# The slot lists of all but five expert steps from a table in device memory, in a one-core mixture-of-experts encoder step

## The chip, the cores and the metric

The kernel runs on one core of a Trainium2 chip. The metric is the device time of one launch in microseconds (us). The three runs of the kernel before took 1218.28, 1220.01 and 1220.52 us, median 1220.01.

## What is computed

One layer of a streaming encoder for 384 tokens: 256 prompt frames and 8 running streams of 16 frames, width 1024, all in float32. An attention mixer with three branches comes first (latent attention, forgetting attention, memory attention, with gates), then a mixture of experts, which this change is about:

```
scores = sigmoid(t @ w_router);  sel = scores + router_bias
top 4 of 8 groups, then the top 8 of the 64 experts in them; w = scores / sum * 2.5
routed = sum over experts e of  gate[:, e] * ((silu(t @ w_gate[e]) * (t @ w_up[e])) @ w_down[e])
y = LayerNorm(ALPHA * x1 + routed + shared expert)
```

Each of the 384 tokens goes to 8 of the 64 experts (hidden width 256), so an expert has 48 tokens in the mean.

## The kernel before, in words

**Order.** `plan()` writes out by hand the order of everything up to the shared expert: projections, attention units, merge, first layer norm, router, shared expert. Each engine walks through this one list and takes its own part. The expert steps come after it, written out in each engine's block. Engines meet only through semaphores.

**Expert steps.** The 64 experts are done two at a time in 32 steps (`PAIRS`), 64 slots for each expert, one slot for each PSUM row. A 33rd step (number `PAIRS`, "quad") takes four chunks of 32 slots for experts with more than 64 tokens; `FIXED` is 33. Further quad steps run only if more than four chunks are needed (`if_more`), which is not so for these inputs. A step n does this:

- **SyncE** (`load_pair`, L608) loads gate, up and down weights of step n, six transfers of 1 MB, into one of two buffer sets. The loads of step n+2 go out, each kind as soon as step n is done with its buffer.
- **GpSimd** (`gather`, L770) fetches the 128 token rows of a step from `x1_dram` with one indirect DMA, whose row numbers are a column of `idx`. It waits on `idx_ready` for that column.
- **TensorE** (`step`, L1198): gate and up products (L1206), the transposes of the rows of the next step (`turn`, L1195), two transposes of the hidden tile (L1213; they wait for `hid_ready`), six products that bring the previous step's result back to token order (L1220), then `slot_tokens` for step n+3 (L932), then the down products (L1231).
- **ScalarE** (`pair`, L1383): silu (L1385), and the scaled copy of the down products (L1390).
- **VectorE** (`pair`, L1833): the hidden tile (L1837), the copies of the transposed rows (`take_turned`, L1831), the copy of the transposed hidden tile (L1841), six additions into `x_sb` (L1858), the matrix `back` (L1845 to L1847), then `copy_slots(n + 3)` (L1580 to L1587) and `build_onehot(n + 4)` (L1566 to L1573).

**Slot lists.** Before a step can gather, it must know which token and which weight sits in each of its 128 slots. Routing gives for each token and expert a position within the expert (`rep`, from `("V", "pos")`). `tgp` holds for each token and expert three numbers: token + 1, weight, position - 1. For step n, `build_onehot` copies the two columns of the step and compares an iota with the position, once for each of the three token tiles; `slot_tokens` multiplies that one-hot matrix with the columns, which sums to the token and weight of each slot; `copy_slots` turns the result into `idx` and `info`. The list of step n+3 is made inside step n. Lists 0 and 1 are made in the plan's `slots` pieces, between those of the shared expert, list 2 just before the loop. `more_chunks` works out which experts need further chunks, and `more_columns` adds their columns to `tgp` (L1556 to L1560).

**Loop.** Steps 0 to 27 run in hardware loops of two steps a turn (`Fori(0, EARLY)`, `EARLY` is 14), the others are unrolled.

Of the kernel before, what the change touches and what calls it, by code (L numbers as in the profile page):

```python
# [33 lines left out]
P = 128  # L34
# [3 lines left out]
TT = 3  # L38
# [14 lines left out]
COLS = E + MORE + 16  # L53
# [14 lines left out]
for _n, _w in (("ident", 128), ("tri", 128), ("ones", 256), ("blk", 128), ("strict", 128), ("causal", 128),  # L68
               ("wfox", 240), ("stack", 64), ("rope", 96), ("iota", MORE), ("tok", 3),
               ("oh", 8), ("eps", 1), ("unused", 1), ("chunks", 10), ("before", 64)):  # L70
    CST[_n] = (_c, _w)
    _c += _w
# [7 lines left out]
def constants():  # L80

    c = np.zeros((P, NCST + T + NMASK), np.float32)
# [9 lines left out]
    masks[:, T + H * 256:] = np.repeat(np.eye(8), P, axis=1)  # L92
# [31 lines left out]
    put("before", np.broadcast_to((np.arange(8)[None, :] < np.arange(8)[:, None]).reshape(1, 64), (P, 64)))  # L124
    return c
# [142 lines left out]
def build(nc, a, outs):  # L268
# [34 lines left out]
    with ExitStack() as ctx:  # L303
# [34 lines left out]
        idx = ctx.enter_context(nc.sbuf_tensor("idx", [P, 8], I32))  # L338
        table = ctx.enter_context(nc.sbuf_tensor("table", [1, 96], I32))
# [104 lines left out]
        counts, chunks, first, more_n = (N.take(1) for _ in range(4))  # L444
        over = N.take(10)
        offs = N.take(MORE)
        since, is_in, begun, shift = (N.take(MORE) for _ in range(4))
        pcol = [N.take(TT, 12) for _ in range(2)]
# [26 lines left out]
        gates_dram = nc.dram_tensor("gates", (GATES, P, T), F32, kind="Internal").ap()  # L475
        x1_dram = nc.dram_tensor("x1_rows", (T, D), F32, kind="Internal").ap()
# [77 lines left out]
        tgp_cleared = sem("tgp_cleared")  # L554
# [4 lines left out]
        more_step = sem("more_step")  # L559
# [47 lines left out]
        def _(sp):  # L607
# [137 lines left out]
        def _(pool):  # L745
# [40 lines left out]
            with pool.Fori(0, EARLY) as i:  # L786
# [17 lines left out]
        def _(pe):  # L804
# [122 lines left out]
            def slot_tokens(n, par, quad=False):  # L927

                w = 12 if quad else 6
# [6 lines left out]
            def more_chunks(k):  # L936
# [6 lines left out]
                elif k == 1:  # L943
                    pe.wait_ge(chunks_ready, 1)
                    mm(ps["S"][1][0:E, 0:1], cc("strict")[0:E, 0:E], chunks[0:E, :], start=True, stop=True).then_inc(chunks_done, 1)
                else:
                    pe.wait_ge(begun_ready, 1)
                    mm(ps["S"][1][:, 0:MORE], cc("ones")[0:E, 0:P], shift[0:E, :], start=True, stop=True)
# [249 lines left out]
            def step(n, q, loaded, quad=False, turned=None, listed=False, lists=None):  # L1198
# [12 lines left out]
                pe.wait_ge(idx_ready, n + 3 if lists is None else lists)  # L1211
# [11 lines left out]
                if listed:  # L1223
                    slot_tokens(n + 3, 1 - q, quad or (isinstance(n, int) and n + 3 >= PAIRS))
# [16 lines left out]
            with pe.Fori(0, EARLY) as i:  # L1241
                for q in range(2):
                    step(i * 2 + q, q, [(q, 32 * (i + 1))], turned=i + 1 + q, listed=True)
            for n in range(2 * EARLY, PAIRS):
                step(n, n % 2, [(n % 2, 32 * (n // 2 + 1))], turned=(n + 1) // 2 + 1, listed=n + 3 < FIXED, lists=min(n + 3, FIXED))
            step(PAIRS, 0, [(0, 32 * (PAIRS // 2 + 1)), (1, 32 * (PAIRS // 2 + 1))], quad=True, lists=FIXED)
            with if_more(pe):
                for n in range(FIXED, FIXED + 2):
                    slot_tokens(n, n % 2, True)
                turn(FIXED, FIXED % 2, FIXED // 2 + 1)  # L1250
                slot_tokens(FIXED + 2, FIXED % 2, True)
# [678 lines left out]
```

## Time and profile before

| | us |
|---|---|
| median of three runs | 1220.01 |
| the profiled execution, its time | 1219.02 |
| its span, first to last instruction | 1216.8 |
| expert steps, first gate product to the last down product | 616.5 to 1193.8 |

The page gives for each engine its busy time and share of the span. TensorE's products are busy for 97% of it, VectorE for 43%, ScalarE for 16%, GpSimd for 4%. The mean granted clock of TensorE is 0.992 of full speed, and 308.95 MB were moved by the 16 DMA engines, 380 GB/s of it in the expert steps. On the chain of work that ended last, TensorE holds 93%. In all rows times are microseconds from the start of the span; "idle before" in square brackets is the time the engine stood still ahead of the instruction, with what ended it.

### The profile page before, as it was taken

The numbers are of one execution on the slowest core, as the hardware profiler recorded it, in microseconds if no ns is written. First come the engines' busy times: TensorE is split into PE (matmuls) and PEld (weight loads), VectorE is DVE, ScalarE is ACT, GpSimd is POOL, SyncE is SP. The second block draws the span as 40 slices with busy tenths as digits, with TensorE's granted clock in tenths as the row PEclk, the third lists the DMA queues.
The fourth block names the chain that finished last, engine by engine and source line by source line (L and its number), as shares of the span: only waits on it lengthen the run. The fifth ranks groups of instructions, "written<-read, shape, count | busy, mean of one in ns | idle before, by whom it ended". The sixth has DMA issues, their size and how long they took to land.

```text
span 1216.8 us, 17670 instructions
## 1 busy us (share of the span) xinstructions
PE 1174.9 (97%) x6510; PEld 678.3 (56%) x6510; DVE 524.6 (43%) x1455; ACT 199.4 (16%) x365; POOL 46.2 (4%) x55
## 2 busy tenths in 40 slices
PE   6999999999999997999999999999999999999994
PEld 4454546666666664545755555555555555555551
DVE  1231014444555642325745445544554454445436
ACT  0212024344433320000100011011101110110011
POOL 0100000000000000001100000000000000000000
PEclk9999999999999998999999999999999999999997
DMA  8431152222264437874259999999999999999981
GB/s 290 143 125 70 69 185 99 80 89 89 89 215 148 156 117 250 333 309 148 84 201 386 382 376 378 400 367 369 380 396 373 379 380 399 378 378 384 375 331 53
DMA packets 84212, 308.95 MB, mean 254 GB/s; under 512 B 14152, under 2 KB 25968, under 8 KB 58040
## 3 DMA queue, kind: packets, MB, share of 16 engines
q1 hardware_dynamic: 67328, 274.96, 57.6%
q0 software_dynamic: 5696, 15.47, 4.4%
q10 hardware_dynamic: 11136, 17.83, 4.2%
q8 instruction: 32, 0.52, 0.2%
q14 instruction: 20, 0.16, 0.0%
HBM read 302.20 MB, written 10.74 MB: 257 GB/s over the span
## 4 chain that ended last, share of the span: by engine, by line
PE 93%; DVE 3%; DMA 1%; issue 0%; ACT 0%; ACTq 0%; DVEq 0%
PE ps_P L1206 19%; PE ps_P L923 10%; PE ps_V L1231 10%; PE ps_V L1220 9%; PE ps_P L829 6%; PE ps_V L1142 5%; PE ps_S L1220 5%; PE ps_T L822 4%; PE ps_P L837 3%; PE ps_V L1151 3%; PE ps_T L1195 3%; PE ps_S L932 2%; PE ps_V L891 1%; PE ps_P L964 1%; PE ps_V L1183 1%; PE ps_S L852 1%
## 5 line engine op out<-in xcount | busy, mean ns | idle before, releaser
L1206 PE MATMUL ps_P<-arena,branch_out 128*64 128x256 f32 (+1 forms) x2176 | 233.6, 379 | 0.6 <-DVE branch_out L1831 0.6
L1206 PEld LDWEIGHTS ps_P<-arena,branch_out 128*64 128x64 f32 (+1 forms) x2176 | 151.2, 135 | 91.0 <-issue 19.2
L923 PE MATMUL ps_P<-xT,weight_ring 128*128 128x384 f32 x384 | 137.0, 491 | 0.0
L1837 DVE TENSOR_TENSOR branch_out<-branch_out,ps_P 128x256 f32<-128x256 f32 x33 | 13.9, 421 | 266.2 <-PE ps_P L1206 266.2
L1220 PE MATMUL ps_V<-weight_ring,branch_out 128*128 128x512 f32 x264 | 124.2, 593 | 0.0
L1231 PE MATMUL ps_V<-arena,branch_out 128*64 128x512 f32 (+1 forms) x544 | 120.6, 599 | 0.0
L1390 ACT ACTIVATE weight_ring<-ps_V,merge 128x512 f32<-128x512 f32 x66 | 45.3, 687 | 427.6 <-PE ps_V L1231 427.6
L1858 DVE TENSOR_TENSOR x_sb<-x_sb,ps_V 128x512 f32<-128x512 f32 x136 | 93.4, 687 | 22.8 <-PE ps_V L1220 17.4
L923 PEld LDWEIGHTS ps_P<-xT,weight_ring 128*128 128x128 f32 x384 | 68.3, 191 | 37.2 <-issue 3.1
L1220 PEld LDWEIGHTS ps_V<-weight_ring,branch_out 128*128 128x128 f32 x264 | 48.0, 192 | 47.3 <-issue 47.3
L1142 PE MATMUL ps_V<-branch_out,weight_ring 128*128 128x384 f32 x192 | 64.1, 497 | 7.4 <-DVE merge L1776 7.0
L1231 PEld LDWEIGHTS ps_V<-arena,branch_out 128*64 128x64 f32 (+1 forms) x544 | 34.8, 135 | 59.5 <-issue 58.9
L1220 PE MATMUL ps_S<-weight_ring,branch_out 128*128 128x512 f32 x132 | 67.4, 592 | 0.0
L829 PE MATMUL ps_P<-weight_ring,xT 128*128 128x512 f32 (+1 forms) x144 | 61.3, 586 | 4.8 <-DMA weight_ring<-w_in 2.9
L1142 PEld LDWEIGHTS ps_V<-branch_out,weight_ring 128*128 128x128 f32 x192 | 37.2, 195 | 34.1 <-issue 9.1
L1372 ACT ACTIVATE merge<-ps_S,small 128x128 f32<-128x128 f32 (+2 forms) x64 | 30.3, 474 | 156.6 <-DVE small L1711 156.4
L1649 DVE COPY merge<-ps_T 128x128 f32<-128x128 f32 (+2 forms) x64 | 27.1, 424 | 61.6 <-PE ps_T L822 61.4
L1858 DVE TENSOR_TENSOR x_sb<-x_sb,ps_S 128x512 f32<-128x512 f32 x68 | 46.6, 686 | 11.3 <-PE ps_S L1220 11.3
L1711 DVE TENSOR_REDUCE small<-ps_S 128x1 f32<-128x128 f32 (+2 forms) x64 | 27.1, 424 | 56.0 <-PE ps_S L853 15.0
L829 PEld LDWEIGHTS ps_P<-weight_ring,xT 128*128 128x128 f32 x144 | 28.0, 197 | 36.1 <-issue 33.7
L1831 DVE COPY branch_out<-ps_T 128x512 f32<-128x512 f32 x66 | 42.5, 685 | 4.6
L1220 PEld LDWEIGHTS ps_S<-weight_ring,branch_out 128*128 128x128 f32 x132 | 25.1, 190 | 31.5 <-issue 31.5
(305 smaller groups left out, 1245.3 us busy)
## 6 DMA issues: line engine op xcount, KB each, us to landing
arena<-w_e_gate SPq DMA_DIRECT2D x68, 1024.0 KB, 8.3
arena<-w_e_up SPq DMA_DIRECT2D x68, 1024.0 KB, 10.7
arena<-w_e_down SPq DMA_DIRECT2D x68, 1024.0 KB, 7.3
weight_ring<-w_in SPq DMA_DIRECT2D x12, 1024.0 KB, 9.2
weight_ring<-w_in ACTq DMA_DIRECT2D x8, 1024.0 KB, 6.1
gates<-arena ACTq DMA_DIRECT2D x24, 192.0 KB, 2.6
xT<-gates ACTq DMA_DIRECT2D x24, 192.0 KB, 7.0
arena<-cache_fox_k SPq DMA_DIRECT2D x8, 512.0 KB, 3.6
```

Source lines behind the costliest of these rows:

```text
L822: return nc.tensor.transpose(out, in_, ident[0:n, 0:n])
L829: last = mm(out[:, 0:w], src[:, k, j * P:(j + 1) * P], slot[:, k % 4, 0:w], start=(k == 0), stop=(k == KD - 1))
L837: last = mm(out[:, 0:T], slot[:, k % 4, m * P:(m + 1) * P], xT[:, k, :], start=(k == 0), stop=(k == KD - 1))
L923: last = mm(out[:, 0:T], slot[:, k % 4, m * P:(m + 1) * P], xT[:, k, :], start=(k == 0), stop=(k == KD - 1))
L1142: last = mm(out[:, 0:T], slot[:, k, m * P:(m + 1) * P], oT[:, br, k, :], start=(k == 0), stop=(k == 3))
L1151: last = mm(out[:, :], yT[:, k, j * P:(j + 1) * P], slot[:, k % 4, :], start=(k == 0), stop=(k == KD - 1))
L1206: last = mm(bank[r:r + wide, 0:256], xgT[q][:, k, r:r + wide], w[h][:, k, :], start=(k == 0), stop=(k == KD - 1))
L1220: mm(tiles[k % 3][:, :], back[1 - q][:, (k // 2) * P:(k // 2 + 1) * P], yo[1 - q][:, (k % 2) * 512:(k % 2 + 1) * 512], start=True, stop=Tr ...
L1231: last = mm(ps["V"][half][r:r + wide, :], hidT[:, m, r:r + wide], ew_down[h][:, m, half * 512:(half + 1) * 512], start=(m == 0), stop=(m = ...
L1390: fn(yo[q][:, half * 512:(half + 1) * 512], ps["V"][half][:, :], ACT.Copy, scale=now_info[:, q, 1:2])\
L1831: V.tensor_copy(xgT[par][:, half * 4:half * 4 + 4, :], ps["T"][half][:, :].rearrange("p (k c) -> p k c", k=4)).then_inc(xgT_ready, 1)
L1858: return V.tensor_tensor(xv, xv, tiles[k % 3][:, :], ALU.add)
```

## The change

- Lists 0 to 4 (`LISTED` = 5) are made as before: 0 and 1 in the plan, 2 ahead of the loop, 3 and 4 in steps 0 and 1. `tgp` shrinks from 172 to 10 columns, and GpSimd's two memsets of it go, with VectorE's wait for them.
- All other lists come from a table in device memory, `slot_rows0` to `slot_rows2`, one for each token tile, with 128 x 59 entries of two floats (slot x step). They are cleared by three SyncE transfers early in the kernel.
- VectorE gets `list_rows()` between `pair(0, 0)` and `pair(1, 1)`: for each token and expert the row of the table (with the further chunks of full experts), the eight rows of each token with `max`, and the eight weights with compare, multiply and reduce.
- GpSimd, after the gathers of steps 3 and 4, issues 24 indirect DMAs (8 for each token tile) that write 128 entries of 8 bytes each. Each waits until the one before it to the same table has landed. Then it loads the three tables into `raw`, 432 bytes for each of 128 partitions.
- At the end of step 2 VectorE waits for these loads (`merge_rows`), adds the three tables, and fixes token numbers. From there `copy_row` copies one column to `idx` in each step, and `slot_tokens`, `copy_slots`, `build_onehot` are no longer called.
- `more_columns` is dropped, `more_chunks` is changed to serve `list_rows`. Steps 0 and 1 are unrolled on TensorE, steps 0 to 3 on VectorE.

```diff
+LISTED = 5
+COLS = 2 * LISTED
+STEPS = LAST + 4
...
+            for j in range(TT):
+                sp.dma_start(rows_dram[j].rearrange("(p s) c -> p (s c)", p=P), a["consts"][:, NCST + T + NMASK:]).then_inc(rows_cleared, 16)
             for n in range(4, 14):
                 w_load(sp, n)
...
-            nc.gpsimd.memset(TGP, 0.0).then_inc(tgp_cleared, 1)
-            pool.wait_ge(tgp_cleared, 1)
-            nc.gpsimd.memset(tgp[:, :, :, 2], -1.0).then_inc(tgp_cleared, 1)
...
             gather(2, 0)
-            with pool.Fori(0, EARLY) as i:
+            gather(3, 1)
+            gather(4, 0)
+            pool.wait_ge(rows_cleared, 16 * TT)
+            pool.wait_ge(rows_ready, 2)
+            for k in range(TOPK):
+                for j in range(TT):
+                    n = j * TOPK + k
+                    if k:
+                        pool.wait_ge(rows_stored[j], 16 * k)
+                    pool.indirect_dma_start(rows_dram[j], bass.IndirectOffsetOnAxis(ap=row_idx[:, n:n + 1], axis=0), entries[:, n, :], None,
+                                            bounds_check=P * STEPS - 1, oob_is_err=False).then_inc(rows_stored[j], 16)
+            for j in range(TT):
+                pool.wait_ge(rows_stored[j], 16 * TOPK)
+                pool.dma_start(raw[:, j, :], rows_dram[j].rearrange("(p s) c -> p (s c)", p=P)[:, 2 * LISTED:2 * STEPS]).then_inc(rows_loaded, 16)
+            with pool.Fori(1, EARLY) as i:
                 for q in range(2):
                     gather(i * 2 + q + 3, 1 - q)
...
-            with pe.Fori(0, EARLY) as i:
+            for n in range(2):
+                step(n, n, [(n, 32)], turned=n + 1, listed=True, lists=n + 3)
+            with pe.Fori(1, EARLY) as i:
                 for q in range(2):
-                    step(i * 2 + q, q, [(q, 32 * (i + 1))], turned=i + 1 + q, listed=True)
+                    step(i * 2 + q, q, [(q, 32 * (i + 1))], turned=i + 1 + q)
...
             def tables():
 
                 dve.wait_ge(free["V"], done_at("V", "pos"))
-                link(V.tensor_scalar(tgp[:, :, 0:E, 2], rep, -1.0, None, ALU.add))
+                link(V.tensor_scalar(tgp[:, :, :, 2], rep[:, :, 0:COLS], -1.0, None, ALU.add))
+
+            def list_rows():
+
+                link(V.tensor_tensor(dest, mask, cc("keys").unsqueeze(1).to_broadcast([P, TT, E]), ALU.mult))
...
+                link(V.tensor_tensor(dest, dest, far, ALU.add))
+                for j in range(TT):
+                    ins = V.max(key8[:, j, :], dest[:, j, :])
+                link(ins)
+                V.tensor_scalar(row_idx[:, :], key8.rearrange("p j k -> p (j k)"), -1.0, None, ALU.add).then_inc(rows_ready, 1)
+                for j in range(TT):
+                    link(V.tensor_tensor(chosen, dest[:, j, :].unsqueeze(1).to_broadcast([P, TOPK, E]),
+                                         key8[:, j, :].unsqueeze(2).to_broadcast([P, TOPK, E]), ALU.is_equal))
+                    link(V.tensor_tensor(chosen, chosen, weight[:, j, :].unsqueeze(1).to_broadcast([P, TOPK, E]), ALU.mult))
+                    link(V.tensor_reduce(weight8[:, j, :], chosen, AX, ALU.add))
...
+            def merge_rows():
+
+                dve.wait_ge(rows_loaded, 16 * TT)
...
+                link(V.tensor_tensor(flat, raw[:, 0, :], raw[:, 1, :], ALU.add))
+                link(V.tensor_tensor(flat, flat, raw[:, 2, :], ALU.add))
+                link(V.tensor_scalar(none, listed[:, :, 0:1], 0.0, 4097.0, ALU.is_equal, ALU.mult))
+                link(V.scalar_tensor_tensor(listed[:, :, 0:1], listed[:, :, 0:1], -1.0, none, ALU.add, ALU.add))
...
-                if listed:
-                    copy_slots(n + 3, 1 - q, quad or (isinstance(n, int) and n + 3 >= PAIRS))
-                if built:
-                    if isinstance(n, int) and n + 4 == PAIRS:
-                        more_columns(0, 4)
-                    build_onehot(n + 4, q, quad or (isinstance(n, int) and n + 4 >= PAIRS))
+                if isinstance(n, int) and n + 3 < LISTED:
+                    copy_slots(n + 3, 1 - q)
+                elif listed:
+                    if isinstance(n, int) and n + 3 == LISTED:
+                        merge_rows()
+                    copy_row(n + 3, 1 - q)
+                if isinstance(n, int) and n + 4 < LISTED:
+                    build_onehot(n + 4, q)
...
-            with dve.Fori(0, EARLY) as i:
+            pair(0, 0)
+            list_rows()
+            for n in range(1, 4):
+                pair(n, n % 2)
+            with dve.Fori(2, EARLY) as i:
```

## Rows read from the trace of the kernel before

**Rows 1.** The page, part 1: busy time of each engine and share of span.
```profile
PE 1174.9 (97%) x6510; PEld 678.3 (56%) x6510; DVE 524.6 (43%) x1455; ACT 199.4 (16%) x365; POOL 46.2 (4%) x55
```

**Rows 2.** The chain that ended last, steps 28 to 30: start, us, what.
```profile
1121.82 3.58 PE ps_V L1231 x16
...
1139.36 3.58 PE ps_V L1231 x16
...
1156.34 3.58 PE ps_V L1231 x16
```

**Rows 3.** The same chain, in steps 1 and 3.
```profile
647.67 0.57 PE ps_S L932 x6
...
677.36 0.24 PE ps_S L1213 x2
```

**Rows 4.** Busy time by stretch: engines, clock, DMA share, GB/s; one late microsecond of a step.
```profile
700.00:800.00 100.00, 100.00 (x636) 56.40 (x635) 45.01 (x126) 10.55 (x18) 5.94 (x6) 1.00 0.95 380
...
844.26:845.26 1.00, 1.00 (x12) 0.50 (x10) 0.00 (x0) 0.45 (x1) 0.26 (x1) 1.00 0.29 90
```

**Rows 5.** DMA issues between 700 and 1100 us: count, size, median us to landing.
```profile
arena<-w_e_up SPq DMA_DIRECT2D x46, 1024.0 KB, 9.8
```

**Rows 6.** Timeline between router and loop: start, us, engine, instruction, idle before.
```profile
592.62 0.41 DVE L1531 TENSOR_SCALAR weight_ring<-merge 128x192 f32<-128x192 f32 x1
...
594.03 0.83 PE L932 MATMUL ps_S<-merge,branch_out 128*128 128x6 f32 x6 [0.87 <-DVE branch_out L1573]
...
606.67 0.46 PE L948 MATMUL ps_S<-merge,cst 64*128 64x92 f32 x2
```

**Rows 7.** Timeline from the end of step 0 on VectorE into step 1.
```profile
632.49 0.69 DVE L1573 TENSOR_TENSOR branch_out<-cst,merge 128x128 f32<-128x128 f32 x3
...
641.31 0.42 DVE L1837 TENSOR_TENSOR branch_out<-branch_out,ps_P 128x256 f32<-128x256 f32 x1 [8.12 <-PE ps_P L1206]
...
642.12 0.40 PE L1213 MATMUL ps_S<-cst,branch_out 128*128 128x128 f32 x2
```

**Rows 8.** Groups of VectorE instructions from 570 us on: busy us, mean ns.
```profile
L1858 DVE TENSOR_TENSOR x_sb<-x_sb,ps_V 128x512 f32<-128x512 f32 x136 | 93.4, 687 | 22.8 <-PE ps_V L1220 17.4 <-PE ps_V L1260 5.4
...
L1519 DVE TENSOR_TENSOR merge<-merge 128x192 f32<-128x192 f32 x1 | 0.4, 358 | 0.0
...
L1477 DVE TENSOR_SCALAR merge<-merge 128x192 f32<-128x192 f32 x1 | 0.3, 260 | 0.6 <-ACT merge L1381 0.6
```

**Rows 9.** Timeline in step 1: the list of step 4, and its gather.
```profile
649.50 0.15 DVE L1586 CAST idx<-merge 128x1 int32<-128x1 f32 x1
...
650.59 0.99 POOL L776 DMA_INDIRECT small<-x_rows,idx  x1 [16.53 <-DVE idx L1586]
```

**Rows 10.** Gathers by tile: the first one (DMA quiet), then those between 700 and 1100.
```profile
DMA to landing us min/median/max: 4.2/4.2/4.2
...
DMA to landing us min/median/max: 3.9/4.5/4.6
```

**Rows 11.** DMA issues between 41 and 48 us: count, size, us to landing.
```profile
s_mla_latent<-lngb POOLq DMA_DIRECT2D x1, 64.0 KB, 1.9
...
p_fox_logf<-small POOLq DMA_DIRECT2D x1, 8.0 KB, 1.9
```

**Rows 12.** Timeline of GpSimd at 44 us: stores one behind the other.
```profile
44.05 0.56 POOL L735 DMA_DIRECT2D s_mla_krope<-small  x1
44.61 0.72 POOL L734 DMA_DIRECT2D p_fox_logf<-small  x1
```

**Rows 13.** The chain around 460 us, where TensorE waits for a load.
```profile
459.62 6.95 DMA xT<-gates
...
467.37 32.83 PE ps_V L1142 x96
```

**Rows 14.** Stretches of 1 us in and after that wait (columns as in rows 4).
```profile
464.00:465.00 1.00, 0.00 (x0) 0.00 (x0) 0.00 (x0) 0.00 (x0) 0.00 (x0) 0.50 1.03 414
...
470.00:471.00 1.00, 1.00 (x3) 0.53 (x2) 0.00 (x0) 0.00 (x0) 0.00 (x0) 0.67 0.63 214
```

More of the change, by code:

```diff
@@ L443, in build @@
         wsum = N.take(TT)
-        counts, chunks, first, more_n = (N.take(1) for _ in range(4))
+        counts, chunks, first = (N.take(1) for _ in range(3))
         over = N.take(10)
-        offs = N.take(MORE)
-        since, is_in, begun, shift = (N.take(MORE) for _ in range(4))
-        pcol = [N.take(TT, 12) for _ in range(2)]
+        since, is_in, begun = (N.take(MORE) for _ in range(3))
+        pcol = [N.take(TT, 6) for _ in range(2)]
+        weight, dest, far, place = (N.take(TT, E) for _ in range(4))
+        chunks_of = N.take(E)
+        token1 = N.take(TT)
+        far_base = N.take(E)
+        raw = R_W[:, 6912:6912 + TT * 2 * (STEPS - LISTED)].rearrange("p (j x) -> p j x", j=TT)
+        none = R_W[:, 7680:7680 + STEPS - LISTED].unsqueeze(2)
+        key8, weight8 = N.take(TT, TOPK), N.take(TT, TOPK)
+        chosen = R_W[:, 6400:6912].rearrange("p (k e) -> p k e", k=TOPK)
+        entries = N.take(TT * TOPK, 2)
         info = N.take(LAST + 4, 2)
@@ L475, in build @@
         gates_dram = nc.dram_tensor("gates", (GATES, P, T), F32, kind="Internal").ap()
+        rows_dram = [nc.dram_tensor(f"slot_rows{j}", (P * STEPS, 2), F32, kind="Internal").ap() for j in range(TT)]
         x1_dram = nc.dram_tensor("x1_rows", (T, D), F32, kind="Internal").ap()
@@ L553, in build @@
         chunks_done = sem("chunks_done")
-        tgp_cleared = sem("tgp_cleared")
+        rows_cleared = sem("rows_cleared")
+        rows_ready = sem("rows_ready")
+        rows_stored = [sem(f"rows_stored{j}") for j in range(TT)]
+        rows_loaded = sem("rows_loaded")
         begun_ready = sem("begun_ready")
@@ L1196, in turn, with step @@
                     last.then_inc(xg_turned, 1)
-            def step(n, q, loaded, quad=False, turned=None, listed=False, lists=None):
+            def step(n, q, loaded, quad=False, turned=None, listed=False, lists=LISTED):
                 pe.wait_ge(xgT_ready, 2 * n + 2)
@@ L1210, in step @@
                 pe.wait_ge(hid_ready, n + 1)
-                pe.wait_ge(idx_ready, n + 3 if lists is None else lists)
+                pe.wait_ge(idx_ready, lists)
                 for m in range(2):
@@ L1872, in _ @@
             with if_more(dve):
-                now[0] = more_step
-                more_columns(4, MORE)
-                for n in range(FIXED, FIXED + 2):
-                    build_onehot(n, n % 2, True)
-                    copy_slots(n, n % 2, True)
-                build_onehot(FIXED + 2, FIXED % 2, True)
+                copy_row(FIXED, FIXED % 2)
+                copy_row(FIXED + 1, 1 - FIXED % 2)
                 take_turned(FIXED, FIXED % 2)
-                copy_slots(FIXED + 2, FIXED % 2, True)
-                build_onehot(FIXED + 3, 1 - FIXED % 2, True)
+                copy_row(FIXED + 2, FIXED % 2)
                 with dve.Fori(0, (LAST - FIXED) // 2) as i:
                     for p in range(2):
-                        pair(i * 2 + p + FIXED, 1 - p, quad=True)
+                        pair(i * 2 + p + FIXED, 1 - p)
                 dve.wait_ge(added, 6 * LAST + 6)
                 dve.wait_ge(back_ready, LAST + 1)
-                now[0] = dve_step
             dve.sem_inc(pairs_over, 1)
```

107 lines of the change are left out of this document (54 added, 53 removed).

## The prediction

> **What bounds the kernel now.** I read the page's first part, then the chain of work that ended last, then single steps in the timeline. TensorE's products are busy for 97% of the span [rows 1], and between 700 and 800 us for all of it, at full clock [rows 4]. The chain runs through TensorE alone there: down products start at 1121.82, 1139.36 and 1156.34 [rows 2]. So a step with a list takes 17.54 us, and step 29 to step 30, between which no list is made, takes 16.98. The chain books 0.57 us for the list's six matmul records in a step [rows 3], which is the same number. VectorE (45 of 100 us) and GpSimd (6 of 100 us) have room [rows 4]. The DMA engines are near their limit: a share of 0.95 at 380 GB/s, but in a late microsecond of the step it is 0.29 [rows 4].
>
> So inside a step only what leaves TensorE counts. Outside, it matters whether the new work, which must be done once and early, is ready when TensorE asks for it.
>
> **What goes.** The products for lists 5 to 32 leave, 28 of them: 28 x 0.57 = **16.0 us**. What VectorE no longer does in a step is worth nothing, since it waits there anyway: it idles 8.12 us before the hidden tile of step 1 [rows 7]. The dropped memsets and `more_columns` were hidden in the same way and count zero.
>
> Between router and loop TensorE waits 0.87 us for the first one-hot, behind routing instructions on 192 columns such as the 0.41 us one [rows 6]. They shrink to 30 columns; I take 0.45 us off. In `more_chunks` a 0.46 us product falls away [rows 6] and one of 64 columns comes in, for which I take 0.2. Together **0.7 us**. The three clearing transfers are issued on SyncE ahead of weight loads that must wait for ring slots anyway: nothing, at worst a few tenths.
>
> **Does the transfer side allow it?** A share of 0.95 of 17.54 us is 16.7 us of transfer work in a step, against a new pitch of 16.97. It fits by a hair, and if it did not, a load of the up weights lands 9.8 us after issue [rows 5] and is needed almost two steps after it. A shortage of a few tenths a step would eat that reserve for all 28 steps before TensorE noticed. I count nothing.
>
> **`list_rows` on VectorE.** Prices [rows 8]: 0.36 us for two-operand work on 192 columns, 0.26 for one operand, 0.69 for 512 columns, plus 0.02 to 0.03 between linked instructions. Seven of the first kind (2.7), three of the second (0.9), three `max` and the cast (0.7), three times three of 512 columns (9 x 0.71 = 6.4), three small ones (0.5): 11.2 us. VectorE is free from 633.18 (632.49 + 0.69) to 641.31, and TensorE could bear 0.5 us more, because the transposes at L1213 begin at about 642.28 by the chain while the hidden tile is done at 641.73 [rows 7]. So step 1 stalls for 11.2 - 8.1 - 0.5 = **2.6 us**. A stall so short should leave the clock alone.
>
> **The table on GpSimd.** This is the term that decides. The list of step 4 comes out of `pair(1)`, now 2.6 us later, and GpSimd issues its gather at 650.59 + 2.6 = 653.2, done at 654.2 [rows 9]. Then come the 24 indirect DMAs. Three prices are not in the trace and are bounded:
>
> - *The pace at which GpSimd issues them.* One takes 0.99 us, and begins 0.94 us after the index is ready (650.59 against 649.65) [rows 9]. If that preparation overlaps with the predecessor the pace is 0.99, if not 1.93. Plain stores from GpSimd stand end to end: 44.05 + 0.56 = 44.61 [rows 12], so their preparation overlaps. I take 0.99.
> - *The landing of a write of 1 KB.* Gathers of 512 KB land after 4.2 us with quiet DMA engines and after 4.5 under the weight loads [rows 10]: the load costs 0.3. Stores of 4 to 64 KB from GpSimd landed after about 1.9 [rows 11], but with an issue of 0.6 to 0.7 us in place of 0.99. So 1.9 is the lower end, 4.5 the upper. I take 1.9 + 0.4 + 0.3, rounded up to 2.7, since it is the size that separates it from a gather.
> - *The chain.* A write waits for the landing of the one before it to its table. One round of three takes the larger of 3 x 0.99 and 0.94 + 2.7 = 3.64 us.
>
> The first lands at 656.9, the eighth to the same table at 656.9 + 7 x 3.64 = 682.4, that of the third table 2.0 later, 684.4. Then the last load of the table, issued 0.3 later and landed 2.2 after that: 686.9. VectorE has stood at the end of step 2 all the while, with the hidden tile of step 3 queued behind it. Five small instructions (1.2 us) and that tile (0.42) bring 688.6. TensorE would have begun its transposes (L1213) at 677.36 [rows 3] + 2.6 - 0.57 = 679.4. Stall: **9.2 us**. While TensorE waited 7 us for a load (459.62 to 466.57) [rows 13], its clock fell to half, and was back only in the stretch at 470, about 3.3 us after it started again at 467.37 [rows 13, 14]. Half of that time is lost: **1.65 us**.
>
> Gather 5 starts only after this, but its rows are needed 17 us later: nothing. `copy_row` is shorter than what it replaces.
>
> **Sum.** -16.0 - 0.7 + 2.6 + 9.2 + 1.65 = -3.3 us. The profiled execution took 1219.02, 1.0 below the median 1220.01; the difference goes onto the median: 1216.7.
>
> **Rivals.**
>
> *Serial issue, slower.* GpSimd prepares an indirect DMA only when the one before is issued, as the gap in front of a gather suggests [rows 9]. Then the pace is 1.93, the 24 take 46.3 us, the last begins at 699.5, lands at 702, the table at 704.3, TensorE resumes at 706.0: a stall of 26.6. Sum -16.7 + 2.6 + 26.6 + 1.65 = +14.2, **1234.2**. For it: every indirect DMA of this trace shows that gap. Against: each of them had just waited for something, and the plain stores show no gap. It turns the sign from a pace of about 1.36 us on (8 rounds of 4.1).
>
> *Landing under load, slower.* The writes land like gathers under load, after 4.5: rounds of 5.44 until about 688, when TensorE stands and the weight loads run out, then 3.64. The eighth round of the third table lands at about 695.6, TensorE resumes at 699.5, stall 20.1: +7.6, **1227.6**. The sign turns at a landing of 3.1 us. The Trainium skill, in "DMA: Bandwidth & Descriptors", section "Latency and other measured facts", gives the memory's latency as 0.2 us in the mean and 2 us at high load, which speaks for this case; the gathers' 0.3 us between quiet and loaded speaks against it [rows 10].
>
> *Quick table, faster.* Landing at 1.9 as the small stores: the pace of 0.99 x 3 rules. Table there at 681.1, TensorE back at 682.8, a stall of 3.4, too short for the clock as I read it [rows 13]. Sum -16.7 + 2.6 + 3.4 = -10.7, **1209.3**. The same page, section "Anatomy of one DMA", puts the fixed part of a DMA from GpSimd at about 2.0 us, whatever its size, which by itself would give this case; the small stores agree with 1.9 [rows 11].
>
> *No gain in the steps.* The transfers do bind and the pitch stays at 17.54: the 16.0 are lost, +12.7, **1232.7**. Against it is the reserve above.
>
> **How the numbers follow.** The forecast case (rounds of 3.4 to 4.0 us) has 0.37, the quick table 0.20, landing under load 0.17, serial issue 0.22, no gain 0.04. The forecast is the likeliest, 1216.7. Of its 0.37 some 0.28 lie more than 0.2% (2.4 us, about what a measurement of this kernel can tell from no change) below 1220.0 and 0.09 within; with 0.19 of the quick table that is 0.47 faster. Within: 0.09, the edges of the quick table and 0.06 of landing under load, 0.16. Slower: 0.37. The range must take in the quick table and serial issue, 1209 to 1234. The forecast's own range, with landings of 2.3 to 3.1 and `list_rows` 1 us either way, is 1213 to 1221.
>
> **What would show it.** The chain should show steps of 16.97 us from step 4 on and no L932 there; 17.54 would prove the transfers. Step 1: an idle of about 2.6 us before L1213, ended by VectorE. Step 3: one of 9 us there, ended by the hidden tile, with VectorE waiting for the load of `raw`. GpSimd's timeline decides between the cases: 24 starts in rounds of 3.6 (forecast), 3.0 (quick), 5.4 (landing), or evenly 1.93 apart (serial). The granted clock should drop to 0.5 once, around 685. The prediction is wrong if the third term is missing because the table is ready before step 3 wants it, or if a stall appears in a place not named here.

## The result, and the profile after

The changed kernel takes **1235.22 us** (median of 4 runs, 1233.39 to 1236.59), the kernel before 1219.32 (4 runs beside them): a ratio of 1.0129 with the interval 1.0111 to 1.0148, 15.9 us slower. The forecast was 1216.7 with a range of 1209 to 1234; the measured time lies above it. The profiled execution took 1234.42 us, its span is 1232.6.

The page of the changed kernel: busy time by engine, which answers to [rows 1], and GpSimd's queue.

```profile
PE 1163.4 (94%) x6342; PEld 657.2 (53%) x6342; DVE 489.2 (40%) x1226; ACT 199.5 (16%) x365; POOL 69.5 (6%) x80
...
q0 software_dynamic: 6560, 15.66, 4.4%
```

TensorE is busy for 11.5 us less and stands still for longer. What it waited for, in the loop (engine, tile, line: total us, times, longest):

```profile
PE ps_S L1243 <- DVE branch_out L1890: 28.3, 3, 25.4
```

Nearly all of it is one wait of 25.4 us. The chain that ended last shows what it consists of (start, us, what):

```profile
645.11 2.93 PE ps_V L1250 x4
648.04 1.34 PE ps_S L1250 x2
649.38 1.72 PE ps_V L1250 x4
...
656.11 6.33 DMA slot_rows<-merge,row_idx
662.49 0.71 issue
663.20 5.74 DMA slot_rows<-merge,row_idx
...
669.71 6.02 DMA slot_rows<-merge,row_idx
...
685.80 5.30 DMA slot_rows<-merge,row_idx
...
702.65 2.11 DMA weight_ring<-slot_rows
705.96 0.43 DVE branch_out L1890
706.43 0.70 PE ps_S L1243 x2
707.13 3.37 PE ps_V L1250 x4
...
1138.19 3.58 PE ps_V L1261 x16
...
1155.15 3.58 PE ps_V L1261 x16
```

Three things are to be read here. The steps: down products start 16.96 us apart, where [rows 2] show 17.54; the saving is there. Step 1: four products take 2.93 us and two take 1.34, while the next four take 1.72: the clock had dropped. And between 656 and 703 the chain runs no longer through TensorE but through GpSimd and its writes of `slot_rows`; the five landings that the chain waits for take 5.3 to 6.3 us from issue, with some 0.7 us before the next write goes out. GpSimd's timeline shows the rounds, three writes each, one to each table (start, us, instruction, idle before it and what ended it):

```profile
654.82 0.99 POOL L792 DMA_INDIRECT small<-x_rows,idx  x1 [20.72 <-DVE idx L1625]
656.11 1.03 POOL L811 DMA_INDIRECT slot_rows<-merge,row_idx  x1 [0.30 <-issue]
657.44 1.00 POOL L811 DMA_INDIRECT slot_rows<-merge,row_idx  x1 [0.30 <-issue]
...
663.20 0.97 POOL L811 DMA_INDIRECT slot_rows<-merge,row_idx  x1 [3.48 <-DMA slot_rows<-merge,row_idx]
...
689.27 0.97 POOL L811 DMA_INDIRECT slot_rows<-merge,row_idx  x1 [2.50 <-DMA slot_rows<-merge,row_idx]
...
700.25 0.97 POOL L811 DMA_INDIRECT slot_rows<-merge,row_idx  x1 [0.30 <-issue]
```

Inside a round two starts are 1.28 to 1.33 us apart but for three places (1.51, 1.69 and 2.04 us, the last two held up by a landing): 0.97 to 1.03 of instruction and 0.30 of idle that nothing but issuing explains. The first five round-to-round distances are 7.09, 6.51, 6.78, 6.35 and 6.43 us. From 691.31 on, when the weight loads have run out behind the standing TensorE, all starts are 1.28 apart. Last, stretches of the same trace (columns as in [rows 4]):

```profile
645.00:646.00 1.00, 1.00 (x3) 0.38 (x3) 1.00 (x3) 0.00 (x0) 0.00 (x0) 0.74 0.99 418
646.00:648.00 2.00, 2.00 (x4) 0.84 (x3) 0.76 (x2) 0.00 (x0) 0.00 (x0) 0.50 1.04 438
...
706.00:710.00 4.00, 3.57 (x6) 1.83 (x7) 2.60 (x6) 0.00 (x0) 1.05 (x1) 0.50 0.26 57
...
800.00:900.00 100.00, 100.00 (x607) 53.43 (x604) 38.30 (x76) 10.55 (x18) 5.95 (x6) 1.00 0.97 391
```

The granted clock is at its lower level, 1.2 GHz, after both stalls, the one of 2.35 us in step 1 as well (it falls in the microsecond from 645, just after TensorE has started again). In the steps the DMA share is 0.97 and the pitch holds.

**The account** against the trace of before, up to the last down product (1209.6 against 1193.8 us, +15.8): -16.0 for the lists; +2.3 for the stall in step 1 and +2.0 for the slow clock behind it (from L1243 at 644.60 to the second half at 649.38 are 4.78 us, where a late step takes 0.24 + 1.72 + 0.86 = 2.82); +25.4 for the stall in step 3 and +2.1 for the clock behind it (0.70 + 3.37 + 0.86 = 4.93 for the same work); together +15.8.

### The profile page after: what moved, and what is told of

The parts are those of the page before. It is cut to its first block, busy times and chain, and to the rows that moved or that the text cites. A ratio compares the mean times of both kernels' runs of the same rounds, so it can differ in the third digit from the quotient of the medians.

```text
span 1232.6 us, 16997 instructions
## 1 busy us (share of the span) xinstructions
PE 1163.4 (94%) x6342; PEld 657.2 (53%) x6342; DVE 489.2 (40%) x1226; ACT 199.5 (16%) x365; POOL 69.5 (6%) x80
## 4 chain that ended last, share of the span: by engine, by line
PE 87%; DVE 5%; DMA 3%; issue 1%; POOL 1%; ACT 0%; ACTq 0%; POOLq 0%; DVEq 0%
PE ps_P L1236 17%; PE ps_P L953 10%; PE ps_V L1250 9%; PE ps_V L1261 9%; PE ps_P L859 6%; PE ps_V L1172 5%; PE ps_S L1250 4%; PE ps_T L852 4%; PE ps_P L867 3%; PE ps_V L1181 3%; PE ps_T L1225 3%; DMA slot_rows<-merge,row_idx 2%; PE ps_V L1213 1%; PE ps_V L921 1%; POOL slot_rows L811 1%
## 5 line engine op out<-in xcount | busy, mean ns | idle before, releaser
L1250 PE MATMUL ps_V<-weight_ring,branch_out 128*128 128x512 f32 x264 | 127.0, 604 | 0.0
```

What stands on the lines that cost most here:

```text
L1250: mm(tiles[k % 3][:, :], back[1 - q][:, (k // 2) * P:(k // 2 + 1) * P], yo[1 - q][:, (k % 2) * 512:(k % 2 + 1) * 512], start=True, stop=Tr ...
```

## The experiments

Ratios are to the kernel before on the same chip. Where no interval stands, the kernel ran once.

**Both stalls from one list.** `list_rows` cut in two, the row numbers ahead of step 0, the weights behind it:

```diff
-            pair(0, 0)
             list_rows()
+            pair(0, 0)
+            list_weights()
```

> list_rows is cut in two: the rows of the table are worked out before step 0, where VectorE idles 5.9 us, the weights after step 0 (6.9 us into an idle of 8.1). Theory (the stall of 2.4 us in step 1 also halved the clock for a while, together 4.1 us, and everything behind it moves as one): no idle before L1243 in step 1, granted clock 1.00 there, gather 4 and the 24 writes begin 4.1 us earlier, the stall in step 3 stays at 25 to 26 us, total 1235.2 - 4.1 = 1231.1 us. Rival (the end of the table is set by something that does not move, such as the time at which the weight loads run out): what step 1 wins is lost again in step 3, total 1235.

1229.93 us, ratio 1.0086 [1.0069, 1.0103]. Its chain:

```profile
642.54 1.72 PE ps_V L1250 x4
...
651.84 5.72 DMA slot_rows<-merge,row_idx
...
700.91 0.70 PE ps_S L1243 x2
```

Step 1 has no stall and its products take 1.72 us. The writes begin 4.3 us earlier (651.84 against 656.11), which is 2.3 + 2.0, TensorE comes back 5.5 us earlier. The total falls by 5.3. That confirms the price of step 1, stall and clock together, and that the table's end moves with its start; the other 1.2 us is the table itself, whose 24 writes took 43.0 us from first start to last (651.84 to 694.79) against 44.1, and the stall there is 24.1 us where 25 to 26 were expected.

**Light weight loads.** Loads of steps 2 to 31 cut to an eighth of their weights; the products run on what is in the tiles, so the kernel leaves seven eighths of those weights out.

```diff
-ew_gate[2 * q + h], w_eg[...]
+ew_gate[2 * q + h][:, 0:1, :], w_eg[...][:, 0:1, :]
```

> The weight loads of steps 2 to 31 are cut to an eighth of their bytes (the steps then use weights that are partly those of steps 0 and 1; all instructions and waits stay). Theory (the weight loads are what makes a write land after 5.4 to 6.3 us instead of 3 or less): the 24 writes go out at the pace of 1.28 us from the first on, in 31 us in place of 45, the table is in SBUF near 690, the stall in step 3 is about 11 us instead of 25.6, total about 1221. Rival (the first writes are slow by themselves, through rows of 8 bytes or through what VectorE and TensorE do meanwhile): rounds of 6.4 to 7.1 us as before, total 1235.

1223.8 us. Timeline of GpSimd at the first and the last write, and of TensorE in between:

```profile
655.09 1.03 POOL L814 DMA_INDIRECT slot_rows<-merge,row_idx  x1 [0.30 <-issue]
...
685.63 0.97 POOL L814 DMA_INDIRECT slot_rows<-merge,row_idx  x1 [0.30 <-issue]
...
683.12 1.41 PE L1239 MATMUL ps_P<-arena,branch_out 128*64 128x256 f32 x2 [1.66 <-issue]
```

The same 24 writes with the same waits take 30.5 us from first start to last, where the changed kernel takes 44.1: with light loads a landing holds a round up only once, by 0.7 us, at the second round, and 1.28 us is the bare pace. So of the 16.6 us by which the table took longer than forecast (44.1 against 27.5), the pace is 3 and the landing under load 13.6. The time was not as expected, though: TensorE's gate products show idle pieces of up to 1.66 us that nothing but issuing explains, and SyncE's next down loads, due at about 676, went out at 689.48, after GpSimd's last transfer (688.6). That came up again.

**Which kind of transfer is slow.** Eight listed steps, so that the table is not waited for; rounds 0 and 4 write 8-byte rows as in the kernel, rounds 1 and 5 read 8-byte rows, 2 and 6 write rows of 512 bytes, 3 and 7 are plain stores. Three quarters of the table are missing, so the later steps gather few tokens; their loads and products are the same.

> Eight lists by one-hot (LISTED 8), and the eight rounds of three DMAs changed to four kinds in turn, all while weight loads run: rounds 0 and 4 the indirect write of 128 x 8 bytes, 1 and 5 an indirect read of 128 x 8 bytes, 2 and 6 an indirect write of 128 x 512 bytes, 3 and 7 a plain store of 1 KB. The table is thus incomplete and the routed experts of later steps get too few tokens. Theory (a write to device memory is slow to be confirmed while the weight loads run, whatever its form): both indirect writes and the plain store land after 5 to 6.5 us, the read after less than 4. Rival A (rows of 8 bytes are the cost): the write of 512 bytes and the plain store land clearly sooner, by 2 us or more. Rival B (it is the indirect form under load): the read is as slow as the write, the plain store lands after 2 to 3 us.

1207.27 us. GpSimd, at the first transfer after each kind:

```profile
661.10 1.03 POOL L822 DMA_INDIRECT read_back<-old_rows,row_idx  x1 [2.98 <-DMA slot_rows<-merge,row_idx]
...
679.09 0.60 POOL L826 DMA_DIRECT2D plain_rows<-merge  x1 [3.44 <-DMA wide_rows<-cst,row_idx]
...
701.02 1.01 POOL L824 DMA_INDIRECT wide_rows<-cst,row_idx  x1 [2.80 <-DMA read_back<-old_rows,row_idx]
```

From the start of a round to the start of the one that waited for it: 8-byte writes 6.6 us (from 654.52), wide writes 7.0 (from 672.07), reads 6.4 (from 694.61), plain stores 7.6 (from 679.09). For the plain stores the profile names no landing as the end of the wait for the first of the three, but it does for the second (680.05 to 688.02). The second pass spreads from 5.7 to 9.7 us and sets no kind apart. All kinds are slow alike under the loads; the expectation that reads come back sooner fell. It is neither the scattered write, nor its small rows, nor the indirect form.

**A later deadline.** Eight steps keep the one-hot; the gathers of steps 5 to 7 go out between the rounds.

```diff
-LISTED = 5
+LISTED = 8
+            gather(4, 0); rounds 0, 1; gather(5, 1); rounds 2 to 4
+            gather(6, 0); rounds 5 to 7; gather(7, 1); the loads
```

> LISTED 8 instead of 5: three more lists by one-hot, the table is first needed at the end of step 5, and the gathers of steps 5, 6 and 7 are put between the rounds of writes. Theory (the whole loss is that the table comes too late for step 3): no stall in step 3, steps of 16.97 us from step 5 on, step 1 as before with its 4.1 us; 25 x 0.57 = 14.3 us saved against the kernel before, total 1219.3 - 14.3 + 4.1 = 1209.1 us. Rival (GpSimd's queue is the new limit): the gathers of steps 5 to 7 come late behind the writes, TensorE waits at L1225 in steps 4 to 6 by 3 us or more each, total 1215 or more.

**1208.76 us**, ratio 0.9913 [0.9895, 0.9931]. TensorE waits 2.3 us in step 1 and nowhere at the table. The writes are as slow as before (6.8 us from round to round at 655.10 and 6.9 at 672.71) and cost nothing. So the whole loss was a deadline: this kernel has three one-hot products more than the changed one (1.7 us) and takes 26.5 us less.

**Two tables for each tile.** If the landing limits a round, twice as many tables should halve it.

```diff
+TABLES = 2
-                    if k:
-                        pool.wait_ge(rows_stored[j], 16 * k)
+                    if k >= TABLES:
+                        pool.wait_ge(rows_stored[t], 16 * (k // TABLES))
```

> The changed kernel with two tables for each token tile (six in all), written in turn, so that a write waits for the one two rounds before it; six loads and three more sums read them back. Theory (the landing of a write under the weight loads is what limits a round): a write now follows its table's last one by 7.7 us of issuing (6 x 1.28) where landing and lag take 6.4 to 7.1, so the pace limits: the 24 writes start 1.28 us apart and take about 31 us (656.1 to 685.6 for the last) instead of 44; six loads instead of three, last landing near 696, TensorE's first product after the stall near 698 to 699 instead of 706.4: about 7.5 us less, 1227.7 us (1225 to 1230). Rival (no more than three of GpSimd's small transfers are in the air, whatever they wait for): the rounds stay at 6.4 to 7.1 us and the time at 1235 or a little above. Rival (the queue moves them at a rate of its own, so that two rounds in the air land twice as late): the writes start 1.28 us apart only at first, and from the third round on a start waits 3 us or more for a landing.

1235.63 us, ratio 1.0131 [1.0116, 1.0147]: no gain at all, and for a reason that none of the three had. The 24 writes do start 1.28 us apart, 655.29 to 684.86, and the six loads of the table are issued by 689.1. But look at the other engines meanwhile (timeline: TensorE, VectorE, SyncE's queue), and at a stretch of it:

```profile
663.39 0.27 PE L1237 MATMUL ps_T<-cst,weight_ring 128*128 128x128 f32 x1 [0.47 <-issue]
...
690.17 0.70 PE L1255 MATMUL ps_S<-cst,branch_out 128*128 128x128 f32 x2 [24.29 <-DVE branch_out L1903]
...
689.69 0.42 DVE L1903 TENSOR_TENSOR branch_out<-branch_out,ps_P 128x256 f32<-128x256 f32 x1 [36.50 <-remote]
...
659.95 1.55 SPq L632 DMA_DIRECT2D arena<-w_e_gate  x2
...
689.62 0.83 SPq L636 DMA_DIRECT2D arena<-w_e_up  x2
```

```profile
670.00:675.00 5.00, 0.00 (x0) 0.00 (x0) 0.00 (x0) 0.00 (x0) 3.78 (x5) 0.50 0.02 1
```

This is step 2, which needs no table. TensorE's products for the hidden tile were done at 662.2; VectorE should have taken them then, as in every step, and began at 689.69, 0.6 us after GpSimd had issued its last transfer. SyncE's next pair of loads was due at about 663.3 and went out at 689.62. TensorE itself ran its last eight transposes with gaps. For 24 us TensorE stood still, and from 670 to 685 nothing moved but GpSimd: DMA share 0.02. The stall had moved from the table into the step before it, with the same length by chance.

**Landing by place in the step.** Two 1 KB stores beside each gather in steps 2 to 13.

> The changed kernel, its table as it is; in steps 2 to 13 GpSimd also stores 1 KB of constants twice with each gather. For even gathers: gather, wait until it has landed, store, wait, store. For odd ones: store, wait until it has landed, gather, wait, store. GpSimd's starts then show how long a gather of 512 KB and a store of 1 KB take, issued where the gathers go out now (as the loads of the next weights have just paused) and some 5 to 12 us later (the loads running). Theory (the landing goes by how much of the weights stands in front at that moment, not by size or form): issued at the gathers' place both are back after 4 to 5 us or less, the small store at about 3; issued later in the step the store takes 6 to 7 from start to the next start, and the gather more than 5. Rival (a wide read is treated otherwise than a small transfer): a gather is back after about 5 us wherever it stands and a small store after 6 to 7 wherever it stands. Time: within 2 us of the changed kernel, 1235, since GpSimd has some 16 us free in each step.

1266.2 us, not 1235, and the test spoilt itself: the stores slow the weight loads (see the last experiments), so every gather came late. What can be read: where gathers followed a store in the running loads, the next transfer, which waited for them, started 8.6 to 10.8 us after them,

```profile
755.62 1.04 POOL L806 DMA_INDIRECT small<-x_rows,idx  x1 [0.30 <-issue]
766.13 0.57 POOL L795 DMA_DIRECT2D small_rows<-cst  x1 [9.47 <-DMA small<-x_rows,idx]
```

against 3.9 to 4.6 to landing at their own place [rows 10]. That speaks against the rival that a gather returns in 5 us wherever it stands, but does not settle it, since the added stores take part. The last run below gives a cleaner reading.

**All of it together.** The split list, two tables, seven listed steps, six writes ahead of gather 4, twelve before gather 5, six after it.

> The listing in two pieces as in the first run, two tables for each tile, seven listed steps, and the writes set around the gathers: rounds 0 and 1 before gather 4, rounds 2 to 5 before gather 5, rounds 6 and 7 after it, the loads after gather 6. Theory: no stall in step 1 (TensorE's gate and up products of step 1 start at 642.1 to 642.3 and the granted clock stays 1.00), none at the table, which is needed near 716 and should stand by 700; 26 of 33 steps without the one-hot product at 0.57 us each: 14.8 us below the kernel before, 1204.5 us (1203 to 1206.5). Rival (writes beside more steps cost the weight loads bandwidth, or the table's writes ahead of gather 4 make that gather late): 1208 or more, with TensorE waiting for x_rows or weights between 650 and 700.

1218.48 us (11 runs), ratio 0.9991 [0.9982, 1.0000]. The missing 14 us are for the most part the same hold-up: against the trace of the seven steps with the rounds kept apart (below), TensorE's down products of step 1 begin 1.4 us later, which was lost ahead of the loop, and those of step 3 14.6 us later, so some 13 us are lost in steps 2 and 3. The first six writes (642.19 to 649.61) disturb nobody, the twelve from 653.19 stop VectorE, the six from 682.38 a little:

```profile
670.63 0.42 DVE L1908 TENSOR_TENSOR branch_out<-branch_out,ps_P 128x256 f32<-128x256 f32 x1 [18.81 <-remote]
...
691.36 0.42 DVE L1908 TENSOR_TENSOR branch_out<-branch_out,ps_P 128x256 f32<-128x256 f32 x1 [10.35 <-remote]
```

The first should have begun near 660, the second near 689.

**Bursts by themselves.** GpSimd's code behind a few gathers of the changed kernel:

```diff
+                if n == 8:
+                    burst("write", 10)
+                if n == 11:
+                    burst("store", 16)
+                if n == 14:
+                    burst("set", 40)
+                if n == 17:
+                    burst("read", 10)
```

> The changed kernel, its table as it is, with bursts that compute nothing put on GpSimd behind a few later gathers: after gather 8 ten indirect writes of 8-byte rows back to back (each to a table of its own, nothing waited for), after gather 11 sixteen plain 1 KB stores back to back, after gather 14 forty short memsets (no DMA), after gather 17 ten indirect reads of 8-byte rows, after gather 20 six indirect writes with four memsets between each and the next, after gather 23 five indirect writes. Theory (indirect DMAs issued back to back by GpSimd for more than about 5 us hold up the other engines' signals: semaphores, SyncE's issues, TensorE's instructions): TensorE shows idle pieces put down to issue and to VectorE, and SyncE's pair of loads takes 1.5 us instead of 0.86, behind gather 8 and gather 17 alone; the memsets and the slower pace show nothing, the five writes little. Rival (any DMA issued without pause does it): the sixteen plain stores as well. Rival (GpSimd's being busy does it): the memsets too. Rival (it was the number of transfers in the air under the weight loads, not the pace): six spaced writes look as ten close ones. Time: 1235 plus 2 to 20 us for each burst that holds the engines up.

1266.08 us. A gather comes 16.97 us after the one before it if nothing holds the step up; the delays are read from the gathers' starts. Each burst stands right behind a gather, which is an indirect DMA too. Ten writes: 748.96 to 776.08, **+10.1**. Ten reads: 924.76 to 950.99, **+9.3**. Forty memsets, 12.8 us long: 0. Six writes 3.0 us apart: 0, read over two gathers. Five writes: +0.3. In the ten writes:

```profile
758.36 0.27 PE L1261 MATMUL ps_T<-cst,weight_ring 128*128 128x128 f32 x1 [0.38 <-issue]
...
765.01 0.42 DVE L1926 TENSOR_TENSOR branch_out<-branch_out,ps_P 128x256 f32<-128x256 f32 x1 [16.93 <-remote]
...
756.35 1.56 SPq L635 DMA_DIRECT2D arena<-w_e_gate  x2
...
845.37 10.66 SPq L643 DMA_DIRECT2D arena<-w_e_down  x2
```

So the hold-up is made by indirect DMAs in a dense row, in either direction; neither GpSimd's being busy nor the spaced writes do it. The light run had at most three writes in the air and showed it, and 24 writes in threes with pauses of some 3 us (the eight listed steps) did not, so it is the pace and not the number outstanding. The sixteen plain stores did nothing to their own step, which spoke for the theory; but two steps later came a delay of 12.9 us (843.95 to 873.84) with the last line shown, loads that took SyncE 10.66 us to issue.

**Seven steps listed, and the rounds kept apart.** The version that came out at 1218.48, without its second tables.

```diff
+            rounds 0, 1; gather(4, 0); rounds 2, 3; gather(5, 1)
+            rounds 4 to 6; gather(6, 0); round 7; the loads
```

> The version of the seventh run without its second tables: the listing in two pieces, seven listed steps, one table for each tile, a round of three writes only when the last has landed, gather 4 after round 1, gather 5 after round 3, gather 6 after round 6. Theory (pauses between the rounds are what keeps the other engines going): the eight rounds take 6.6 us each and run from 642 to 695 with the gathers between, the table stands at about 705 and is needed at about 713; no stall of TensorE in steps 1 to 5 over 1 us, clock 1.00 there; 26 steps at 0.57 us: 14.8 below the kernel before, 1204.8 us (1203 to 1207). Rival (three tokens' lists fewer in the loop cost the same wherever the writes go; beside five steps they take the weights' bandwidth): 1208 or more.

**1204.55 us** (1204.12 to 1205.08), ratio 0.9874 [0.9857, 0.9890]. Page and chain:

```profile
PE 1161.8 (97%) x6354; PEld 658.1 (55%) x6354; DVE 491.9 (41%) x1244; ACT 199.4 (17%) x365; POOL 70.3 (6%) x80
```

```profile
642.44 1.72 PE ps_V L1264 x4
...
660.17 1.72 PE ps_V L1264 x4
...
677.72 1.72 PE ps_V L1264 x4
...
695.35 1.72 PE ps_V L1264 x4
```

TensorE is back at 97% of the span and in the chain throughout; its steps follow at 17.73, 17.55 and 17.63 us while the 24 writes go out beside them (640.82 to 692.49). It is 15.8 us faster than the kernel before and 30.7 faster than the changed one, with the same work in another order but for two more one-hot lists. Against the 1218.48 us of the version with second tables it shows what the pauses are worth, some 13 us: the same seven listed steps and the same split list, with a pause after every three writes. Gathers that left late (gather 5 at 668.60) did no harm.

**Rows, and the stores again.**

> The burst kernel again with other bursts: after gather 8 ten indirect writes of 16 rows instead of 128, after gather 11 and again after gather 23 fourteen plain stores, after gather 17 seven indirect writes of 128 rows. Theory A (each of the 128 rows is descriptors that somebody must write, and that writing is what crowds the other engines out): the ten narrow writes hold nobody up, the seven wide ones (9 us) cost a few us, 3 to 6, between the 0.3 of five and the 10 of ten. Theory B (the indirect form itself does it, whatever the rows): the ten narrow writes cost 5 us or more, like the wide ones. The stores: SyncE took 10.66 us for a pair of loads some 35 us after the sixteen stores of the last run, and TensorE stood for 8.3 us; if the stores cause that, it comes again behind one or both of the bursts here; if it was an accident, behind neither. Time by A without the accident: 1235 plus 3 to 6.

1266.66 us. Ten writes of 16 rows: no delay (750.33 to 767.33). Seven of 128 rows: none either (911.29 to 928.28), where theory A said 3 to 6 us; VectorE took its hidden tile on time, at 919.70, in the midst of them. Theory B is out; A is left with its first half and a step between seven and ten that I can't explain. It also takes the weight from the six spaced writes above, since seven dense ones pass as well; what pauses do is shown by the 24 writes of the eight and the seven listed steps. The stores: behind both bursts TensorE waited for weights again, gathers late by 8.2 us (835.20 to 860.37) and by 18.9 over two (1030.10 to 1082.97). It was no accident. The loads in the stretch after a burst, against the one before it:

```profile
795.00:800.00 5.00, 5.00 (x16) 1.98 (x16) 4.12 (x8) 0.00 (x0) 0.00 (x0) 1.00 1.01 424
...
810.00:815.00 5.00, 5.00 (x19) 2.61 (x18) 4.35 (x8) 0.00 (x0) 0.00 (x0) 1.00 1.35 114
815.00:820.00 5.00, 5.00 (x25) 1.81 (x25) 1.96 (x6) 1.04 (x2) 1.06 (x1) 1.00 0.84 54
```

14 KB of stores turn the core's 424 GB/s, nearly all of it weight loads, into 54 to 145 for some 30 us, with DMA engines that count as busy. That is another effect than the hold-up: it comes later and shows first in the loads' rate, and the indirect DMAs have none of it (beside the ten reads of the burst kernel the loads' queue moved 3.66 MB from 925 to 935, beside the writes of the two-table run 1.99 MB from 660 to 665).

The same trace answers what the landing by place left open. After the first stores the loads never catch up: from 860 to 912 they land 20 to 24 us after issue in the median, in the changed kernel 7 to 10, and their short pause at the gather is gone (401 to 451 GB/s in each of the four microseconds from 894; in the changed kernel 418, 197 and 229 from 885.9). The ten gathers from 860.37 to 1013.12, two of them with a burst right behind, landed after 8.3 to 8.6 us; the 22 of the changed kernel between 733 and 1090 after 4.0 to 4.8, and the five of this run ahead of its stores after 4.2 to 4.4. So a gather under loads that do not pause takes twice as long, which puts its quick return down to the pause.

## Why the prediction was wrong

Point by point, in its own order.

- *Lists leave the steps, 16.0 us.* Right: 16.96 us a step. The transfers allow it, with a DMA share of 0.97 at 391 GB/s, as its reserve argued, and "no gain in the steps" is out.
- *Prologue, 0.7 us.* The stretch from the first merge operation (579.95) to the first one-hot (594.10) is 0.45 us shorter, as I had it for that part; but the loop begins at 616.49 against 616.53. The stretch before it came 0.5 later in this execution. Nothing is to be seen in the total.
- *`list_rows`, 11.2 us and a stall of 2.6.* Right: 632.9 to 644.2, TensorE stood 2.35.
- *"A stall so short should leave the clock alone."* Wrong: 0.74, then 0.50 until 648, +2.0 us. The rows for it were one wait of 7 us [rows 13, 14] and said nothing on short ones. So the clock fell twice, not once as the signs had it. The split run showed clock and stall gone together.
- *Pace 0.99.* Wrong: 1.28. Plain stores from GpSimd stand end to end; indirect DMAs leave 0.30 us between them. My rival of 1.93 was wrong too: the preparation overlaps but for that third of a microsecond. Priced by the light run, the pace cost 3.0 us.
- ***The landing of a write, 2.7 us, with 4.5 as the upper end.*** This is the step that failed. Under the loads it took 5.3 to 6.3, and a round 6.4 to 7.1 instead of 3.64. The mistake was in the bound, not only in the choice: I took 4.2 quiet against 4.5 loaded from the gathers [rows 10] as the price of load, 0.3 us. But a gather leaves just as the loads pause (a share of 0.29 in that microsecond [rows 4]), and the table's writes leave at any time. Where the pause was missing, gathers took 8.3 to 8.6 us (the last run), so their 4.5 was no upper bound. My reason to go below the gathers, size, did not count either: rows of 8 and 512 bytes took 6.6 and 7.0 us to the next start. The Trainium skill, "DMA: Bandwidth & Descriptors", section "Anatomy of one DMA", puts the fixed part of a DMA from GpSimd at about 2.0 us; the quiet parts of the traces agree (1.9 [rows 11], and 2.11 for the table's load), under the loads it is short by 3.3 to 4.3 us. On the same page, section "Latency and other measured facts", the Trainium skill has the memory's latency rise from 0.2 us to 2 at high load; that is the right sign and too little of it for what the writes showed.
- *Stall of 9.2 in step 3.* 25.4. The first write started 1.9 later than forecast, the 24 took 16.6 longer, the table's loads 0.8 less, and TensorE's own arrival was 1.6 later, for the slow clock in step 1: 1.9 + 16.6 - 0.8 - 1.6 = 16.1 of the 16.2 between the two.
- *Clock afterwards, 1.65.* 2.1 measured.

The time of 1235.2 lies beside that of the rival "serial issue" (1234.2), but that is luck: a pace of 1.93 us is not what happened; "landing under load" was the right mechanism with too short a landing. The place of the loss was named. The sign of the whole was missed: by the prediction's own sum it turns at a landing of 3.1 us, and I had put the landing at 2.7.

What was shown and what not: that the weight loads make the landing long (light loads, 44.1 to 30.5 us), that the deadline makes it cost (1208.76 and 1204.55), and that step 1 cost 4.3 us with its clock and 5.3 in the total (split). That gathers are quick for the pause in the loads they meet is shown by the last run (4.0 to 4.8 us with it, 8.3 to 8.6 without); whether anything else that the stores leave behind takes part was not tried. By what way a dense row of indirect DMAs holds up the other engines stays open, as does the threshold: five writes cost 0.3 us and seven nothing, ten did not pass, twelve neither, and six that began 14 us after the twelve had ended cost 2 us. Why stores of 8-byte rows slow the loads was not tried further.

## What to carry to other kernels

The price of a transfer under load must be read from rows that were issued into the load, not from ones that happen to leave in its pauses; look at the DMA share in the microsecond of issue before calling a row an upper bound. A chain of small dependent DMAs beside saturated loads costs some 6.5 us a link here (6.4 to 7.1 in the changed kernel) whatever it carries, so put its deadline links x 6.5 us away, which cost 0.57 us per listed step, rather than make it shorter. And do not make it shorter by taking its pauses out: GpSimd's indirect DMAs in a dense row stop the other engines.

## What the hardware showed that was not expected

- Ten indirect DMAs of 128 rows from GpSimd, 1.28 to 1.30 us apart, delay the step beside them by 9 to 10 us: VectorE takes the finished products, and SyncE issues the next up loads, only after the row has ended (765.0 against 762.8, and 940.8 against 938.8), and TensorE runs with gaps of 0.2 to 1.0 us. Seven such DMAs, ten with 16 rows each (1.15 us apart), and 24 in threes with pauses of some 3 us between delay nothing.
- Fourteen plain 1 KB stores (8 bytes a partition) in 7.5 us cut the core's DMA traffic from 424 GB/s to between 54 and 145 for about 30 us, at a DMA share of 0.7 to 1.4. Two of them in each of twelve steps, with the gathers they delayed, cost 31 us.
- After a TensorE idle of 2.35 us the granted clock went from 1.00 to 0.50, and 2.0 us were lost by it; in the split run, without that idle, the same products ran at full pace.
- Under weight loads that do not pause a gather of 512 KB took 8.3 to 8.6 us to land, against 4.0 to 4.8 where the loads dip as it leaves.
